# Attention probabilities turned by a scaling matrix, and gated branch parts summed from PSUM

## The reference

```
s = einsum("bqkgd,btkd->bkgqt", qi, k)
w = softmax(s, axis=-1)
o = einsum("bkgqt,btkd->bqkgd", w, v)
...
g_f, g_m, g_g = split(sigmoid(gate_logits + b_gate), 3)
mix = (g_f * y_f + g_m * y_m + g_g * y_g) @ w_o
```

## Time and profile before

| | us |
|---|---|
| median of 3 runs | 3033.32 (3033.26 to 3038.99) |
| the profiled execution | 3038.01 |
| its span | 3036.2 |
| TensorE busy in it | 2899.3 (95%) |
| GpSimd, ScalarE, VectorE busy | 1812.8, 1269.8, 972.7 |

### The profile page before, as it was taken

The page is one execution under the profiler, slowest core; times in us unless marked ns, Lnnn a source line. Parts: engine busy times, 40 slices in busy tenths (PEclk is TensorE's granted clock), DMA queues, the critical chain, the costliest instruction groups (busy, mean ns, idle before and its releaser), DMA issues.

```text
span 3036.2 us, 49296 instructions
## 1 busy us (share of the span) xinstructions
PE 2899.3 (95%) x20391; PEld 2567.5 (85%) x20391; DVE 972.7 (32%) x1757; ACT 1269.8 (42%) x1675; POOL 1812.8 (60%) x1380
## 2 busy tenths in 40 slices
PE   6999989999999999999999998999999999899999
PEld 4875758867888686798998998989999998889999
DVE  3133243341132433342344313245322214144321
ACT  2434543333222335543444345455444435455543
POOL 1411125524455241485985988648897997846896
PEclk8999999999999999998999999999999999999999
DMA  6444343313222145453544565435555556534553
GB/s 217 104 130 148 119 131 97 97 42 111 97 96 96 44 111 166 133 168 117 181 168 139 180 174 161 153 84 175 172 180 167 180 180 159 163 98 139 180 180 126
DMA packets 397420, 422.63 MB, mean 139 GB/s; under 512 B 74577, under 2 KB 367433, under 8 KB 396957
## 3 DMA queue, kind: packets, MB, share of 16 engines
q1 hardware_dynamic: 397246, 420.11, 44.5%
HBM read 419.01 MB, written 3.16 MB: 139 GB/s over the span
## 4 chain that ended last, share of the span: by engine, by line
PE 83%; POOL 6%; DVE 5%; ACT 3%; issue 2%; DMA 1%; SPq 1%; DVEq 0%; POOLq 0%; ACTq 0%
PE ps L827 63%; PE ps L811 17%; POOL ring_r L1643 6%; PE ps L854 2%; ACT ring_hi L1676 1%; DVE stat L2626 1%; DVE arena L2640 1%; DMA ring<-in_w_in 0%; SPq L595 0%; PE ps L1322 0%; DVE arena_r L2864 0%; DVE arena L2920 0%; DMA ring<-in_ffn_w_up 0%; DVE arena_r L2722 0%; SPq L561 0%
## 5 line engine op out<-in xcount | busy, mean ns | idle before, releaser
L1643 POOL TENSOR_TENSOR ring_r<-ring,ring_hi 128x512 fp32r<-128x512 f32 x1376 | 1812.6, 1355 | 1200.9 <-ACT ring_hi L1676 1200.8
L827 PE MATMUL ps<-hT_r,ring_hi 128*128 128x256 f32 (+1 forms) x6176 | 1147.3, 309 | 36.4 <-POOL ring_r L1643 21.6
L827 PEld LDWEIGHTS ps<-hT_r,ring_hi 128*128 128x128 f32 x6176 | 927.3, 195 | 111.3 <-issue 47.6
L1676 ACT ACTIVATE ring_hi<-ring 128x2048 fp32r<-128x2048 f32 x344 | 655.0, 1910 | 366.2 <-DMA ring<-in_ffn_w_down 110.0
L827 PE MATMUL ps<-hT_r,ring_r 128*128 128x256 f32 (+1 forms) x3088 | 695.4, 307 | 0.0
L827 PE MATMUL ps<-arena_r,ring_hi 128*128 128x256 f32 (+1 forms) x3504 | 588.4, 309 | 9.5 <-DVE arena_r L2722 3.8
L827 PEld LDWEIGHTS ps<-arena_r,ring_hi 128*128 128x128 f32 x3504 | 501.7, 192 | 44.7 <-DVE arena_r L2722 4.5
L827 PEld LDWEIGHTS ps<-hT_r,ring_r 128*128 128x128 f32 x3088 | 509.7, 195 | 23.7
L827 PE MATMUL ps<-arena_r,ring_r 128*128 128x256 f32 (+1 forms) x1752 | 330.7, 308 | 0.0
L827 PEld LDWEIGHTS ps<-arena_r,ring_r 128*128 128x128 f32 x1752 | 263.7, 191 | 15.8
L811 PE MATMUL ps<-arena 128*64 128x128 f32 (+9 forms) x1616 | 195.0, 354 | 7.2 <-DVE arena L3030 2.3
(11 more groups left out here) (297 smaller groups left out, 2340.3 us busy)
## 6 DMA issues: line engine op xcount, KB each, us to landing
ring<-in_w_in SPq DMA_DIRECT2D x82, 1024.0 KB
ring<-in_w SPq DMA_DIRECT2D x64, 1024.0 KB
ring<-in_w_ada SPq DMA_DIRECT2D x48, 1024.0 KB
ring<-in_ffn_w_up SPq DMA_DIRECT2D x44, 1024.0 KB
ring<-in_ffn_w_gate SPq DMA_DIRECT2D x44, 1024.0 KB
ring<-in_ffn_w_down SPq DMA_DIRECT2D x44, 1024.0 KB
ring<-in_w_in SPq DMA_DIRECT2D x48, 256.0 KB
ring<-in_w_o SPq DMA_DIRECT2D x8, 1024.0 KB
```

What stands on the lines that cost most here:

```text
L827: last[t] = pe.matmul(o, lhsT, rhs, start=start and j == 0, stop=stop and j == n - 1, skip_group_check=True)
L1643: ins = pool.tensor_tensor(k.ring_lo[s][:, part], k.ring[s][:, part], k.ring_hi[s][:, part], ALU.subtract)
L1676: act.activation(k.ring_hi[s][:, :], k.ring[s][:, :], ACT.Copy).then_inc(k.hi_ready[s], 1)
```

## The change

In the attention the probabilities are no longer multiplied by one over their row sums. VectorE forms, for each head of a unit, the 128x128 diagonal matrix of these factors (the identity times a factor per row) and TensorE multiplies the raw exponentials by it in place of the transposition with the identity: one ordinary fp32 product does both. VectorE forms the diagonals of unit u-1 at the start of round u, ahead of the copy `moved(u - 3)` and of the maxima of u.

In the gated sums the product of gate and branch stays in its PSUM tile, and the add reads it there; the bank is free after the add. ScalarE rounds each pair of tiles when its two sums are there (it waits for the banks, no longer for `gated`), and VectorE makes the low part of the third pair after the seventh tile.

```diff
-PROB, PROBT, ROT, OG = 0, 2048, 0, VM
+PROB, PROBT, DIAG, ROT, OG = 0, 2048, 3072, 0, VM
...
+        diag = area(DIAG, 2, 2, P)
...
-                                mm = flip(ps[:, b, t * P:t * P + P], prob[:, (u - LAG) % 2, a, t * P:t * P + P])
+                                mm = products(ps[:, b, t * P:t * P + P],
+                                              [(prob[:, (u - LAG) % 2, a, t * P:t * P + P], diag[:, (u - LAG) % 2, a, :])])
...
-                            mixed_half(0, cols)
-                        skip(4)
+                            mixed_half(0, cols, summed)
+                        summed = [T.take() for _ in range(4)]
...
-                act.wait_ge(S["gated"], T.next("gated", 4))
                 for j in range(2 * c, 2 * c + 2):
+                    act.wait_ge(k.bank_done[summed[3][0]], summed[3][1])
+                    for tile in summed[2 * (j % 2):2 * (j % 2) + 2]:
+                        act.wait_ge(*k.moved(tile))
...
-                def probabilities(u):
-                    buf, n = u % 2, HALVES[todo[u][1]][1]
+                def scaling(u):
+                    buf = u % 2
                     dve.wait_ge(*k.moved(score[u][1]))
                     rsum = k.stat[:, 8 * buf + 2:8 * buf + 4]
                     dve.reciprocal(rsum, rsum).then_inc(S["dve_step"], 1)
                     dve.wait_ge(S["dve_step"], T.next("dve_step"))
                     for a in range(2):
-                        p = prob[:, u % 2, a, 0:n]
-                        ins = dve.tensor_scalar(p, p, rsum[:, a:a + 1], None, ALU.mult)
+                        ins = dve.tensor_scalar(diag[:, buf, a, :], ident, rsum[:, a:a + 1], None, ALU.mult)
                     ins.then_inc(S["prob_ready"], 1)
...
                     if LAG <= u:
                         skip(2)
+                    if 1 <= u <= len(todo):
+                        scaling(u - 1)
                     if u >= 4 and u % 2 == 0:
                         moved(u - 3)
                     if u < len(todo):
                         maxima(u)
-                    if 1 <= u <= len(todo):
-                        probabilities(u - 1)
...
-                tm = area(TMP_M, TOK)[:, cols]
+                added = {}
...
                             mixed_low(0, cols)
+                            mixed_low(1, cols)
...
-                            dve.tensor_tensor(tm, gate(t)[:, cols], ps[:, b, 0:n], ALU.mult) \
-                                .then_inc(k.bank_read[b], 1)
-                            dve.wait_ge(*k.moved(T.last()))
-                            step = "dve_step" if g == 1 else "gated"
-                            dve.tensor_tensor(m, m, tm, ALU.add).then_inc(S[step], 1)
-                            dve.wait_ge(S[step], T.next(step))
-                mixed_low(1, cols)
+                            dve.tensor_tensor(ps[:, b, 0:n], gate(t)[:, cols], ps[:, b, 0:n], ALU.mult) \
+                                .then_inc(S["dve_step"], 1)
+                            if g == 2:
+                                dve.wait_ge(*k.moved(added[4 * c + t]))
+                            dve.wait_ge(S["dve_step"], T.next("dve_step"))
+                            dve.tensor_tensor(m, m, ps[:, b, 0:n], ALU.add).then_inc(k.bank_read[b], 1)
+                            added[4 * c + t] = b, v
+                            if (c, g, t) == (1, 2, 2):
+                                mixed_low(2, cols)
+                mixed_low(3, cols)
```

More of the change, by code:

```diff
@@ L338, in __init__ @@
             "mods_ready", "squared_qk", "normed", "latent_rounded", "rstd_ready", "roped", "row_max", "prob_ready",
-            "branch_rounded", "branch_split", "gated", "mixed_rounded", "mixed_split", "relu_ready", "hid_rounded", "hid_split",
+            "branch_rounded", "branch_split", "mixed_rounded", "mixed_split", "relu_ready", "hid_rounded", "hid_split",
             "hid_used",
@@ L400 @@
     0, 1024, 2048, 3072, 4096, 4608, 5120, 7168, 7680, 8192, 9216, 11264, 13312, 15360, 17408)
-PROB, PROBT, ROT, OG = 0, 2048, 0, VM
+PROB, PROBT, DIAG, ROT, OG = 0, 2048, 3072, 0, VM
 SQ_CKV, SQ_CQ, SQ_QG, SQ_KG, STD_KV, STD_KG = OM, OM + 1024, VM, FIN + 1536, FIN + 512, FIN + 1024
-FIN_HI, OM_HI, OG_HI, MIXED, TMP_M, GATES = DFT1, 0, 2048, QN, VG, FIN
+FIN_HI, OM_HI, OG_HI, MIXED, GATES = DFT1, 0, 2048, QN, FIN
 MIXED_HI = 0
@@ L1956, in branches, with mixed_half @@
                         if (c, g) == (1, 2):
-                            mixed_half(0, cols)
-                        skip(4)
-            def mixed_half(c, cols):
-                act.wait_ge(S["gated"], T.next("gated", 4))
+                            mixed_half(0, cols, summed)
+                        summed = [T.take() for _ in range(4)]
+                return summed
+            def mixed_half(c, cols, summed):
                 for j in range(2 * c, 2 * c + 2):
+                    act.wait_ge(k.bank_done[summed[3][0]], summed[3][1])
+                    for tile in summed[2 * (j % 2):2 * (j % 2) + 2]:
+                        act.wait_ge(*k.moved(tile))
                     two = slice(2 * j, 2 * j + 2)
@@ L1966, in mixed_half, with mix_out @@
                         .then_inc(S["mixed_rounded"], 1)
-            def mix_out(l, cols):
-                mixed_half(1, cols)
+            def mix_out(l, cols, summed):
+                mixed_half(1, cols, summed)
                 split()
@@ L2057, in _ @@
                 heads(cols)
-                branches(l, cols, attention(l, cols))
-                behind = mix_out(l, cols)
+                summed = branches(l, cols, attention(l, cols))
+                behind = mix_out(l, cols, summed)
                 modulate_tokens(plain, cols, modulated(mod + SC2, mod + SH2, halves), behind[1])
@@ L2708, in branches, with mixed_low @@
                             dve.wait_ge(*k.moved(((b + 4) % BANKS, T.value(f"bank{(b + 4) % BANKS}"))))
-                            dve.tensor_tensor(tm, gate(t)[:, cols], ps[:, b, 0:n], ALU.mult) \
-                                .then_inc(k.bank_read[b], 1)
-                            dve.wait_ge(*k.moved(T.last()))
-                            step = "dve_step" if g == 1 else "gated"
-                            dve.tensor_tensor(m, m, tm, ALU.add).then_inc(S[step], 1)
-                            dve.wait_ge(S[step], T.next(step))
-                mixed_low(1, cols)
[L2717 to L2723, removed]
+                            dve.tensor_tensor(ps[:, b, 0:n], gate(t)[:, cols], ps[:, b, 0:n], ALU.mult) \
[8 more added lines that the diff above has]
+                mixed_low(3, cols)
+            def mixed_low(j, cols):
+                two = slice(2 * j, 2 * j + 2)
+                dve.wait_ge(S["mixed_rounded"], T.next("mixed_rounded"))
+                dve.tensor_tensor(mixed_split[1][:, two, cols], mixed[:, two, cols], mixed_split[0][:, two, cols],
+                                  ALU.subtract).then_inc(S["mixed_split"], 1)
             def residual(tile, b, cols, halves, g):
```

## The result

The changed kernel takes 3053.56 us (median of 5 runs, 3052.37 to 3059.17) against 3037.0 for the kernel before in the same session (5 runs, 3033.26 to 3038.99): ratio 1.0062, 95% interval 1.0047 to 1.0077. The forecast, slower at 3048 in 3024 to 3062, holds in sign and range. Some of its terms don't hold in size, as is shown further down. The profiled execution took 3053.56 us with a span of 3051.7; before it was 3038.0 and 3036.2.

What follows compares the result with a forecast made beforehand. TensorE, busy 95% of 3036.2 us, was taken as the bound. 32 - 30.8 - 12 + 25 + 5 - 4.6 = +14.6 us on 3038.0 gave 3052.6, or 3048 as a median; range 3024 to 3062.

Steps and rivals of the forecast that it cites:

- 2 to 4, half clock: TensorE's lower clock: -12 us in the attentions, +5 behind new waits, -2.6 at the second layer's end.
- Term 1: Attention: 320 turns as fp32 products cost 0.10 us more each in TensorE's stream, +32 us (31 to 36).
- the control row: Second block: eight turns take 0.93 us, eight fp32 products of the same form 1.71; 0.0975 more for each.
- its sign: Attention turns: 16 instructions in 1.7 to 1.8 us where 8 took 1.0; wrong if not 0.21 us each.
- Term 2: Attentions: TensorE's waits go, -30.8 us, and the 23.9 us worked at half clock, -12 us.
- three or so: New attention waits that may bring the lower clock back, 1.7 us lost each: +5 us (0 to 13).
- The condition that the prediction set: Attentions: after a TensorE wait of 2.0 us or more the lower clock may come again.
- Term 3: Attentions: TensorE waits for the attended pair's copy, late behind exponentials and scaling: +25 us (8 to 35).
- Term 4: Gated sums, second layer's end: the 3.81 us low-part wait becomes 1.0 + 0.8; -4.6 us (0 to -6.4).
- The waits really go: Rival: attended copy not in the way, clock stays up; 3018 to 3027 us, say 3024; chance 0.26.
- Its point of decision: The faster rival decides as soon as the attentions' new waits for the copy stay below 15 us together.
- Worse clock: Rival: lower clock after most of nine waits, GpSimd meets scalings oftener; 3058, up to 3066 us; chance 0.16.

Runs made afterwards that it cites:

- copy_first: The changed kernel with VectorE's copy of the attended pair moved ahead of forming the diagonals (copy, scaling, maxima): 3032.93 us, ratio 0.9986 to the kernel before.
- order_alone: The kernel before with its wide scaling of the probabilities put ahead of the copy and the maxima, turns still transpositions: 3064.12 us, ratio 1.0093.
- gated_alone: The kernel before with only the gated sums of the change: 3033.12 us, ratio 0.9977.
- attention_only: The changed kernel with the old gated sums, so only the two attention edits: 3061.73 us, ratio 1.0082 to the kernel before.
- scaling between: VectorE's order copy, scaling, maxima in each round; as the only change to the kernel before: 3015.24 us, ratio 0.9926.
- flip_scale_first: The kernel before with the wide scaling ahead of copy and maxima, plus the new gated sums: 3056.96 us, ratio 1.0067.

## Why the prediction came out as it did

Between the cuts the prediction's terms against the trace:

| term | predicted | traced |
|---|---|---|
| 1, turn as a product | +32 | +39 |
| 2, waits of the earlier trace rows that go | -30.8 | -30.7 |
| 3, waits for the copy in their place | +25 | +21.3 |
| 2 to 4, half clock (-12, +5, -2.6) | -9.6 | -5.1 |
| 4, wait for the low part | -2.0 | -2.2 |
| sum | +14.6 | +22.3 (cuts: +22.6) |

**Term 1 was mis-sized**, and beyond its own range of 31 to 36. I took 0.10 from the control row as the difference of starts, 1.71 - 0.93 for eight. In an attention each set of turns stands between attended products and scores. The transpositions take 1.02 there, as the rows at 270.92 and 271.94 showed, and the 16 instructions of the products 1.99, 0.28 more than in the control: a set of products pays more on its way in and out, and the control was read as if it had the same neighbours. The prediction named 1.7 to 1.8 us and 0.21 each as its sign; at 1.99 and 0.25 this term is wrong by it. In the control the next form started 31 ns behind the last product and the second instruction 111 ns behind the first; in the attention it is 205 and 213. An estimate by the Trainium skill's rule (page "TensorE: Matmul & The Clock Gate", section Terms, transpose mode four times faster for FP32) gives 3 x 0.109 = 0.33 us more a turn. The trace disagrees: 0.12. The rule's factor does not hold for this form, where both kinds load 128x128 weights and move only 128 columns.

**Term 2**: the mechanism was right for the waits. For the clock it was wrong to book the whole 23.9 us as gained and then to add back 5 for "three or so" new waits. The lower clock came at four of the new waits, for 23.8 us. Between the cuts 34.1 us at half clock became 23.8, and half of that difference is the 5.1 of the table. The condition that the prediction set, a wait of 2.0 us or more, fits the kernel before: its six waits of 2.04 to 3.81 us between the cuts have a stretch at half clock around or within 1.5 us behind them, and the shorter ones, up to 1.61, have none. It does not carry over to the changed kernel, where 1.40 and 1.74 had one and the 2.23 at 443.52 had none. That waits bring the lower clock fits `copy_first`, with 8.2 us idle and 3.4 at half clock, and `order_alone`, with 45.4 and 75.1; but idle time alone does not give the half clock: `gated_alone` has 35.9 and 23.9, the change 25.2 and 23.8.

**Term 3 was right in mechanism, place and nearly in size.** The wait came in even rounds 14, 22, 24, 26, 28, 30 and 32 of the first layer, and 16 of the second, at 1.3 to 2.2 us (named: 1.6 to 2.7), in 18 and 20 at 1.64 and 1.40 (named: 1.8), and in round 10 of the second at 2.49 (named: 3.3). `copy_first` moves just the copy, and 21 us go between medians, a part of them by the clock (between the cuts 17.0 us of idle time, and 20.4 us less at half clock). `order_alone` makes the chain longer and TensorE's filling shorter, and the one wait that was followed grows by just the sum of the two.

**Term 4 was right**: predicted waits 1.0 + 0.8, traced 0.98 + 0.65; predicted -4.6 us, alone -5.6 and within attention_only's comparison -6.5. On the two forms of the add, the Trainium skill's page "SBUF — State Buffer" (section Who interferes with whom) and the rows agree again: beside a GpSimd instruction 1.07 us with both inputs in SBUF, 0.42 with one in PSUM. With GpSimd at rest the old add takes 0.42 as well, in the kernel before:

```profile
1347.67 0.42 DVE L2713 TENSOR_TENSOR arena<-arena 128x256 f32<-128x256 f32 x1
```

**The forecast's place.** Between the cuts the sum is 8 us low. Between medians the change is +16.6 and the sum 2.0 low; another 3.7 are the level, since five runs of the kernel before have their median at 3037.0 and the three that were shown at 3033.3. Where the 6 us between +22.6 and +16.6 come from isn't settled: in one execution each, the parts outside the cuts differ by several us. That the time came out within 6 us of the forecast is partly luck, and no credit to term 1 and the clock, which were 7.0 and 4.5 us too low.

**The rivals.** "The waits really go" is what scaling between does. Its point of decision was put rightly: with the copy out of the way, term 3 stays far below 15 us, and `copy_first` is 4.5 us faster than before. The rival said 7.4 to 15 faster, with 32 us for the turns, which add 39. "Worse clock" did happen in `order_alone`, whose waits for the copy go up to 3.97 us. What stays open is how the lower clock would have to be priced beforehand: the same program's executions differ by 17 us with it (`flip_scale_first`), and I have no rule from these traces that gives the length of a stretch from the wait ahead of it.

## What to carry to other kernels

When work is moved forward in an in-order queue, ask of each instruction that it is moved past who waits for that one. Here a copy of 0.42 us that frees a PSUM bank was put behind a wait for exponentials, which cost 21 us; the scaling put behind that copy and ahead of the maxima gains 23 us in the kernel before. What an edit adds to an engine's stream is not yet its price: the turn as a product, 39 us of TensorE's time, cost 20.8, 20.5 or nothing by the waits around it. Read the price of a new instruction form in its real surroundings, handovers included, and count lower clock that waits cause as gone only where no waits of that length are left.

## What the hardware showed unexpectedly

- Eight fp32 products of 128x128 weights and 128 columns take 1.99 us between instructions of other forms (start to start 213 + 14 x 112 + 205 ns), eight transpositions 1.02 (164 + 6 x 109 + 203). Between transpositions and products with 256 columns the same eight products took 1.71. A product is twice a transposition here, since it is two instructions at the pace of one.
- A stretch at half clock can last 34.2 us with TensorE busy for 30.7 of them, with two waits of 1.45 us inside it. A wait of 1.61 us elsewhere had none behind it.
- VectorE's two 128x128 scalings take 0.48 us alone, and beside GpSimd up to 2.33, nearly what two 512-wide ones take there (2.79), here in the second layer of the changed kernel:

```profile
1225.93 2.33 DVE L2645 TENSOR_SCALAR arena<-const,stat 128x128 f32<-128x128 f32 x2
```
